# Activations in two layouts 128 bytes apart modulo 256, one tile for the meta keys' probabilities, and their scaling on ScalarE

## What is computed

```python
def hybrid_layer(x, ...):                      # twice
    h = rms_norm(x, norm_g)
    q, k, v, gate_a, u_b, gate_b, q_idx, k_idx, w_idx, merge = split(h @ w_in)
    q, k = rope(rms_norm(q)), rope(rms_norm(k)); q_idx, k_idx = rope(q_idx), rope(k_idx)
    # per query: score = sum_h relu(q_idx . k_idx) * w_idx, keys of later chunks masked,
    # the best 64 keys are kept; softmax over them, 8 heads of 64; times v
    attn = indexer_sparse_attention(q, k, v, q_idx, k_idx, w_idx, 64)
    y_a = (attn * silu(gate_a)) @ w_a
    y_b = (multiscale_pool(u_b) * silu(gate_b)) @ w_b
    return x + (sigmoid(m_a) * y_a + sigmoid(m_b) * y_b) @ w_out

def second_block(x, mem, ...):
    h = h + 0.5 * swiglu(rmsnorm(h), w_gate_up, w_down)
    u = rmsnorm(h); p = u @ w_in               # then short conv, Mamba-2 branch, gates
    h = h + (g_a * (y_a @ w_out_a) + g_b * (y_b @ w_out_ssm)) @ w_mix_out
    h = h + memory_cross_attention(rmsnorm(h), rmsnorm(mem), w_q, w_kv, w_o)
    h = h + 0.5 * swiglu(rmsnorm(h), w_gate_up, w_down)
    return rmsnorm(h)
```

## The kernel before, in words

| feed | step between tiles | high to low copy |
| --- | --- | --- |
| `n0`, `n1` (layers) | 64 | 0 |
| `f1` (first feed-forward) | 128 | 0 |
| `mx` (mixer) | 128 | 0 |
| `x` (cross attention) | 0 | 128 |
| `f2` (second feed-forward) | 0 | 0 |
| `yy`, in the layers | 64 | 0 |
| `yy`, elsewhere | 0 | 0 |

## Time and profile before

### The profile page before, as it was taken

How to read it: one execution, slowest core, us unless ns; L and a number is a source line. 1 busy time by engine, 2 the same in 40 slices (tenths; PEclk the granted TensorE clock), 3 DMA queues, 4 the chain that set the end, 5 groups by cost and what they waited for, 6 DMA issues and landing times.

```text
span 1240.8 us, 22233 instructions
## 1 busy us (share of the span) xinstructions
PE 1223.4 (99%) x8794; PEld 1128.8 (91%) x8794; DVE 620.0 (50%) x1461; ACT 717.6 (58%) x1344; POOL 979.9 (79%) x774
## 2 busy tenths in 40 slices
PE   7999999999999999999999999999999999999998
PEld 6999899998889888889999999999999988888886
DVE  5476754456756444412756678742135235444411
ACT  6455646465556666645645677774447437666642
POOL 5666768767568999989789767779889758898895
PEclk9999999999999999999999999999999999999999
DMA  7334435434335555555456555545556425555552
GB/s 255 137 137 142 148 121 186 153 138 168 113 128 199 189 187 187 189 184 187 158 207 214 180 167 181 181 160 187 178 179 224 167 104 183 206 187 186 185 184 106
DMA packets 59911, 213.31 MB, mean 172 GB/s; under 512 B 6656, under 2 KB 6944, under 8 KB 59680
## 3 DMA queue, kind: packets, MB, share of 16 engines
q1 hardware_dynamic: 57456, 207.67, 48.0%
q10 hardware_dynamic: 2352, 4.23, 1.2%
HBM read 210.79 MB, written 1.08 MB: 171 GB/s over the span
## 4 chain that ended last, share of the span: by engine, by line
PE 96%; DVE 2%; ACT 1%; DMA 0%; issue 0%; SPq 0%; DVEq 0%
PE bank L388 19%; PE bank L361 18%; PE bank L362 17%; PE bank L363 17%; PE bank L391 10%; PE bank L1474 2%; PE bank L1473 2%; PE bank L1472 2%; PE bank L905 1%; PE bank L709 1%; PE bank L915 1%; PE bank L1920 1%; PE bank L847 1%; PE bank L2278 1%; PE bank L2280 1%; PE bank L2279 1%
## 5 line engine op out<-in xcount | busy, mean ns | idle before, releaser
L321 POOL TENSOR_TENSOR wlo<-raw,whi 128x512 fp32r<-128x512 f32 x770 | 979.7, 1302 | 248.1 <-ACT whi L313 246.6
L313 ACT ACTIVATE whi<-raw 128x1024 fp32r<-128x1024 f32 x387 | 405.1, 1053 | 54.1 <-DMA raw<-w_dram 29.5
L361 PE MATMUL bank<-xx,whi 128*128 128x256 f32 (+1 forms) x1296 | 377.3, 291 | 8.4 <-DVE xx L454 8.4
L362 PE MATMUL bank<-xx,whi 128*128 128x256 f32 (+1 forms) x1296 | 368.7, 284 | 0.0
L363 PE MATMUL bank<-xx,wlo 128*128 128x256 f32 (+1 forms) x1296 | 367.7, 284 | 0.0
L361 PEld LDWEIGHTS bank<-xx,whi 128*128 128x128 f32 x1296 | 246.1, 190 | 15.1 <-issue 11.0
L362 PEld LDWEIGHTS bank<-xx,whi 128*128 128x128 f32 x1296 | 245.6, 189 | 1.5 <-issue 1.0
L363 PEld LDWEIGHTS bank<-xx,wlo 128*128 128x128 f32 x1296 | 245.1, 189 | 0.0
L388 PE MATMUL bank<-xx,whi 128*128 128x512 f32 x704 | 177.2, 393 | 0.0
L388 PEld LDWEIGHTS bank<-xx,whi 128*128 128x128 f32 x704 | 126.5, 189 | 22.6
L361 PE MATMUL bank<-yy,whi 128*128 128x256 f32 (+1 forms) x502 | 145.0, 289 | 0.0
(11 more groups left out here) (292 smaller groups left out, 1520.6 us busy)
## 6 DMA issues: line engine op xcount, KB each, us to landing
raw<-w_dram SPq DMA_DIRECT2D x387, 512.0 KB, 3.3
ar<-sums_dram ACTq DMA_DIRECT2D x16, 256.0 KB, 3.9
ar<-mem_dram SPq DMA_DIRECT2D x1, 1024.0 KB, 6.3
out_dram<-ar SPq DMA_DIRECT2D x4, 256.0 KB, 2.2
cst<-con_dram SPq DMA_DIRECT2D x1, 721.0 KB, 9.1
h<-x_dram SPq DMA_DIRECT2D x2, 272.0 KB, 4.6
h<-x_dram SPq DMA_DIRECT2D x1, 544.0 KB, 5.9
ar<-fin_dram SPq DMA_DIRECT2D x1, 512.0 KB, 4.3
```

Source lines behind the costliest of these rows:

```text
L313: e.activation(whi[:, i % NSPL, :], raw[:, i % NRAW, :], ACT.Copy).then_inc(*whi_done.done(i))
L321: return e.tensor_tensor(wlo[:, q, c0:c1], raw[:, i % NRAW, c0:c1], whi[:, q, c0:c1].bitcast(F), ALU.subtract)
L361: e.matmul(o, wh, both[:, 0, :], start=(i == 0), stop=False)
L362: e.matmul(o, wh, both[:, 1, :], start=False, stop=False)
```

## The change

1. **Layouts.** `xx` and `yy` change place. The new steps and distances, in bytes modulo 256: `n0` 64 and 64; `n1` 64 and 128; `f1` 128 and 0 as before; `mx` and `x` 128 and 128; `f2` 128 and 0; `yy` 128 between its two copies, and outside of the layers also 128 between tiles (`y_both` puts odd tiles in a second half, 12·256 + 32 elements on). Where activations stand (`last_tile`, the memory's norm) they are read through `ys`, with the old step 256 and distance 6144. The cross attention's output uses step 288. With that, each narrow matmul of `mx`, `x` and `yy` starts 128 bytes modulo 256 away from the one before. `xx` shrinks from 5376 to 4672 columns, `yy` and the constants grow, and the tensors behind them move.
2. **Meta keys.** The 16 meta keys of all 8 heads go into one tile `K.LM` [128, 8·16] that is transposed once per query tile (step 6) and multiplied in step 7 by `K.VZ` [128, 8·64], the meta values spread block by block over the heads, in four matmuls of 128 columns. `VZ` is made once per layer by one small matmul with a constant (`C_REP`) and one DVE multiplication with a mask (`C_HM`).
3. **Pairs.** The transposes of a pair of heads share one PSUM bank, and ACT takes them out in one instruction (256 or 512 columns) into a single `PT` buffer.
4. **Scaling.** The multiplication by the reciprocal moves from DVE (L966) to ACT: for each head one activation over the ordinary keys in place and one over the 16 meta keys into `LM`.

```diff
-YCOLS = 24 * 256
-XCOLS = 5376
+YCOLS = 24 * 256 + 32
+XCOLS = 4672
...
-        "n0": Norm("n0", "ng0", rows[0], cols3[0], 0, h, xx, T),
-        "n1": Norm("n1", "ng1", rows[1], cols3[1], 0, h, xx, T),
+        "n0": Norm("n0", "ng0", rows[0], cols3[0], 0, h, *stepped(T, 8 * T + 16)),
+        "n1": Norm("n1", "ng1", rows[1], cols3[1], 0, h, *stepped(T, 8 * T + 32)),
         "f1": Norm("f1", "f1n", rows[0], cols3[0], Z, h, *stepped(288, 2304), Z),
-        "mx": Norm("mx", "mxn", rows[1], cols3[1], Z, h, *stepped(288, 2368), Z),
-        "x": Norm("x", "xn", rows[0], cols3[0], Z, h, *stepped(320, 2592), Z),
-        "f2": Norm("f2", "f2n", rows[1], cols3[1], Z, h, *stepped(320, 2688), Z),
+        "mx": Norm("mx", "mxn", rows[1], cols3[1], Z, h, *stepped(288, 2336), Z),
+        "x": Norm("x", "xn", rows[0], cols3[0], Z, h, *stepped(288, 2336), Z),
+        "f2": Norm("f2", "f2n", rows[1], cols3[1], Z, h, *stepped(288, 2304), Z),
...
     def y_both(i):
-        return yy[:, :, i * S:(i + 1) * S]
+        at = i // 2 * S + i % 2 * (12 * S + 32)
+        return yy[:, :, at:at + S]
...
+        e.matmul(o[:, 0:64], cst[0:META, C_REP:C_REP + 128], K.V[0:META, 2, 0:64], start=True, stop=True).then_inc(
+            *piece.done("vz", l))
...
+                for i in range(nn):
+                    for q in range(2):
+                        m = e.matmul(ob[64 * q:64 * q + 64, 128 * j:128 * j + 128], K.V[:, i, 0:64], pt[:, nn * q + i, :],
+                                     start=(i == 0 and j == 0), stop=False, skip_group_check=True)
...
+            if s == 7:
+                e.wait_ge(*v_step.of("vz", l))
+                e.wait_ge(*s_out.of("pm", l, t))
+                for j in range(4):
+                    m = e.matmul(ob[:, 128 * j:128 * j + 128], K.VZ[:, 128 * j:128 * j + 128], K.PM, start=False, stop=True,
+                                 skip_group_check=True)
...
+                for q in range(2):
+                    e.wait_ge(*s_step.of("p", l, t, 2 * j + q))
+                    for i, k0 in enumerate(firsts):
...
+                        m = e.transpose(o[:, at:at + 128], K.L[:, 2 * j + q, k0:k0 + 128], ident)
...
+            if s == 6:
...
+                e.wait_ge(*s_step.of("lm", l, t, 7))
+                e.transpose(o[:, 0:128], K.LM, ident).then_inc(*piece.done("pm", l, t))
...
-                e.activation(pt[0:16, 0, :], o[0:16, 0:128], ACT.Copy).then_inc(*s_out.done("pt0", l, t, hh))
-                e.activation(pt[:, 1:nn, :], o[:, 128:128 * nn].rearrange("p (a b) -> p a b", b=128), ACT.Copy).then_inc(
-                    *s_out.done("pt", l, t, hh))
+                e.activation(pt[:, 0:n, :], o[:, 0:128 * n].rearrange("p (a b) -> p a b", b=128), ACT.Copy).then_inc(
+                    *s_out.done("pt", l, t, j))
...
+            for hh in (2 * s - 4, 2 * s - 3) if 2 <= s < 6 else ():
+                x, r = K.L[:, hh, META:nk], K.rs[:, hh:hh + 1]
+                e.wait_ge(*v_step.of("rs", l, t, s - 2))
+                e.activation(x, x, ACT.Copy, scale=r).then_inc(*s_step.done("p", l, t, hh))
+                if t:
+                    e.wait_ge(*piece.of("pm", l, 0))
+                e.activation(K.LM[:, META * hh:META * hh + META], K.L[:, hh, 0:META], ACT.Copy, scale=r).then_inc(
+                    *s_step.done("lm", l, t, hh))
...
-                for hh in (2 * s - 4, 2 * s - 3):
...
-                    e.tensor_scalar(x, x, K.rs[:, hh:hh + 1], None, ALU.mult).then_inc(*v_step.done("p", l, t, hh))
```

123 lines of the change are left out of this document (71 added, 52 removed).

## The result

The change gained 7.8 us where I had forecast 17.3:

| | before | after |
| --- | --- | --- |
| median | 1242.29 us (4 runs, 1242.18 to 1243.21) | 1234.46 us (4 runs, 1234.00 to 1234.56) |
| ratio | | 0.9933, 95% interval 0.9918 to 0.9949 |
| span of the profiled execution | 1240.8 us | 1232.5 us |

What follows compares the result with a forecast made beforehand. TensorE, busy 99% of the span, was taken as the bound. From 1242.63 us, layouts 7.7, attention 5.2, waits 2.0 + 1.5 + 0.7, less 0.2, gave 16.9 gained: 1225.7, forecast 1225 with the median 0.4 lower; range 1217 to 1236.

Steps and rivals of the forecast that it cites:

- a sign of being wrong: Attention: the prediction is wrong if TensorE waits for ScalarE's scaling by more than 2 us in all.
- rival (c): Attention: transposes wait for ScalarE, 0.5 us in 6 to 12 steps; 1229 to 1232, up to 1237; chance 0.12.
- (d): Attention: the same wait for ScalarE at 1.5 us in 12 steps, plus clock falls; slower, 1250 us; chance 0.03.
- term 2.1: Products reading `yy` outside the layers: 690 matmuls, each 3.1 ns nearer to the next, 2.1 us gained.
- The layers' term: Matmuls in the two layers: 996 of 256 columns at 0.8 ns, 1452 of 272 at 0.4, 1.4 us gained.
- the mixer's: Stage `mx`: 1944 matmuls from 118.5 to 116.9 ns, by extending a line over place changes; 3.1 us gained.
- rival (b): Layouts: the place modulo 256 isn't what matters, or costs elsewhere what it gives; attention alone, 1233 to 1235; chance 0.13.
- The wide blocks: Rounds of wide matmuls in the second feed-forward and those reading `yy`: 0.005 to 0.02 us a round, 1.0 us gained.
- 5.2 + 2.0 + 1.5 + 0.7: Attention gains in us: matmuls net 5.2, shorter stall in layer 1 2.0, no clock fall 1.5, other transpose waits 0.7.
- twelve steps s = 4 to 6: Attention: 0.62 us a step from values (0.40) and two fewer transposes (0.22), 7.4 us; transposing `LM` costs 0.4.
- The rival price: Attention's values: if 16-row pieces slip in cheaply, they gain 3.8 us instead of 6.4, making the sum 2.6 higher.
- Start-up: 0.2 us lost by forecast: Start: the constants' load grows by 70 KB beside weights, costing 0 to 0.4 us, taken as 0.2.

Runs made afterwards that it cites:

- e7: The kernel before with only the scaling of probabilities moved from VectorE to ScalarE: 1240.24 us, ratio 0.9979.
- e10: The kernel after plus 48 unused matmul sequences behind its last product, varying places of moving columns and weights and widths; the time as a whole says nothing.
- e5: The kernel after plus 47 unused matmul sequences behind its last product, differing in places and in the matmul ahead; about 280 us more as a whole.
- e6: The kernel after plus unused attention pieces (old and new forms) and 512-column matmuls in several layouts behind its last product; the time as a whole says nothing.
- e15: The kernel after run once more, unchanged: 1234.58 us, ratio 0.9932.
- e2: The kernel before with the attention part of the change alone, constants included, layouts as before: 1237.06 us, ratio 0.9953.
- e11: The kernel after without alternation: outside the layers moving columns at place 64 modulo 256 bytes, the last product's standing activations at 192: 1230.47 us, ratio 0.9905.
- e12: As e11, but with the last product's standing activations back at place 128: 1229.88 us, ratio 0.9893.
- e13: As e12, plus six 16-column matmuls, each just ahead of a block that begins a long stretch, results overwritten: 1225.52 us, ratio 0.9866.
- e14: As e13, plus 18 unused float32 products of zeros before the first input and 7 ahead of the first norm's sums: 1225.56 us, ratio 0.9860.
- e3: The kernel before with the whole of `yy` moved 128 bytes further on, nothing else changed: 1243.95 us (one run).
- e1: The kernel before with the layout part of the change alone, attention and constants as before: 1237.87 us, ratio 0.9957.

## Why the prediction was half wrong

**Right.** Attention was the larger gain of the two in fact, and the stall's cause was the one named: with the scaling off VectorE's queue the wait went from 1.43 to 0.57 us in e7 (0.30 in after) and the clock fall behind it is gone. ScalarE didn't become a bound: the transposes waited 1.3 us in six places for its scaling, in the view of the earlier trace rows, where they had waited 1.4 in two for VectorE's, and the steps are some 0.9 us longer than without waits. That is under the 2 us named as a sign of being wrong, so rival (c) is small, and (d) is out. `yy` at 116.7 ns is the forecast value in the one stage where it came.

**Layouts: 7.7 us forecast, 3.5 to 4 measured.** In the stage of slots 253 to 281, 2.0 us came in after and e10, 0.6 in e5, e6 and e15. Of the 2.0, 1.6 are `yy`'s (term 2.1) and 0.4 belong to the eight slots there that read `xx`, 118.9 ns before and 116.7 after. The layers' term (1.4) came as about 1.1. The term that fell is the mixer's: 1944 matmuls at 1.6 ns, 3.1 us, and 0.8 came, those eight slots included: their mean went from 118.5 to 118.1 ns, not to 116.9. Its step was "going on in the line gives 116.6": I had read 120.0, 118.5 and 117.6 as a function of how many transitions change place. They are means over rhythms. One layout has several (116.7, 118.3 and about 118.8 ns for the alternating one), and the mixer fell mostly into the slower ones, in the traces of after, e10 and e15 alike. That `yy` came to 116.7 in the first of them was luck. The earlier trace rows showed it: 117.9 and 119.2 for one layout. I quoted that under rival (b) and gave it 0.13, where it was evidence against taking any one distance per layout. The wide blocks (1.0) came as about 0.5: the second feed-forward gained 0.6, while the 512-column matmuls on `yy`, whose two halves now lie 128 bytes apart, went from 231 to 233 ns. Rival (b) would have said 1233 to 1235; the number is there, but by luck: its mechanism, that places don't matter or give back elsewhere what they gain, isn't what the runs show.

**Attention: 9.4 us forecast (5.2 + 2.0 + 1.5 + 0.7), 6.5 measured in e2.** By terms, from starts of blocks in the trace after: the twelve steps s = 4 to 6 gained 5.2 us, `LM` included, where 7.4 - 0.4 stood. Part is the price (0.53 instead of 0.62 without waits, e6), part are new waits in three steps of t = 0, 0.53 us in one of them. The four steps s = 7 lost 2.2 us, 1.9 forecast. The steps s = 3 with the stall and the other waits gained 3.2, 3.6 forecast. The clock gave 1.3 of 1.5. Making `VZ` cost 0.54 and 0.53, not 0.4 each. The rival price drawn from the Trainium skill's section "The mechanism" (0.24 a step for the values) fails too: e6 has 0.36. It was a misreading, since the 16 rows lie within the 128 of the matmuls around them, and the section has loads overlap only where the row groups differ.

**Start-up: 0.2 us lost by forecast, 1.7 measured** (2.28 less the 0.54 of `VZ`, which layer 0 makes there). No term of mine covered it, and it isn't a term of the change as far as the traces tell: over those of this study, less `VZ` where it is made, slot 5 came from 0.1 us sooner to 1.9 us later than in the profile of before. That profile has the second best start of all. I should have asked how much of its span was luck, and had no second trace to ask.

The range 1217 to 1236 did hold the time. Of the 9.5 us that are missing, about 4 are the layouts', where a small distance from one or two places was multiplied by a large count; about 3 are attention's, above all a price 0.09 us too high and waits put at nothing in 12 steps; and 1.5 to 1.7 are the start-up.

## What to carry to other kernels

Before a distance between matmuls is multiplied by a count, read it in several stretches of one layout: if it differs there, it is a rhythm, and its place in the program matters as much as the addresses. Where operands' places can be chosen, measure the difference of moving and standing place for each width by sequences behind the kernel; that took two runs and found a better layout than the change had. Then run the program more than once: the same stretch can fall into another rhythm. Compare kernels by the start of each slot of weights: one subtraction then tells luck in the start-up from the change.

## What the runs showed of the hardware

- Where no place changes, a 256-column matmul follows the last one after 113.3 to 120.0 ns, by the difference modulo 256 bytes of the places of moving columns and weights: 120.0 at 0, 113.3 or 117.8 at 192 (e5, e10). The Trainium skill, "TensorE: Matmul & The Clock Gate", section "Back-to-back issue gap", gives 109.2 ns for an isolated matmul of this width at full clock, with no word of places; no steady sequence here came under 113.3.
- With 512 contiguous moving columns difference 0 is the best one: 227.7 ns, with 232.0 at 128 and 233.5 at 192 (e10), and 226.7 at 0 against 232.6 and 233.3 at 128 with activations standing (e6).
- The distance has several steady values for one layout, each held for up to 695 matmuls. What stands just ahead takes part in the choice, but the same program also fell into different ones in two executions (e11 and e12, after and e15). Behind a 16-column matmul of about 0.11 us (837.27 - 836.93 in e13, where 0.23 stood) the faster one came in six of six places in e13 and in five of six in e14.
- The same wait of 1.4 us at one place of layer 1 was followed by half the clock for 3.4 us in before and e3 (0.57 of a window of 4) and for 6.8 in e1, 1.5 us more of time. Behind 0.57 us at that place there was no fall (e7), behind 0.60 us in the start-up there was one (after).
- Twelve float32 instructions of which four have 16 rows take 0.95 us with nothing else at work, eight of 128 rows 0.59 (e6). The Trainium skill, "TensorE: Matmul & The Clock Gate", section "The mechanism", has a weight load overlap a running matmul only where the row group differs, which it doesn't here (the 16 rows are among the 128 of their neighbours), and the trace agrees: the 16-row ones cost 0.36 us together, and the first 128-row one starts 0.20 us behind the last 16-row one.
